# Attention on one Trainium2 core: value products of selected and sliding keys issued in one run, the compressed product last

## The reference

```python
s = jnp.einsum('bqgre,bige->bqgri', qg, kc) * SCALE
p_cmp, _ = _masked_softmax(s, (cmp_last[None, :] <= t[:, None])[:, None, None, :])
o_cmp = jnp.einsum('bqgri,bige->bqgre', p_cmp.astype(vc.dtype), vc)
...
o_slc = jnp.einsum('bqgrk,bqgke->bqgre', p.astype(vs.dtype), vs)
...
o_win = jnp.einsum('bqgrk,bkge->bqgre', p.astype(vw.dtype), vw)
...
o = g[..., 0:1] * o_cmp + g[..., 1:2] * o_slc + g[..., 2:3] * o_win
```

## Time and profile before

| | |
|---|---|
| time, median of 3 runs | 2013.63 us (2011.82 to 2014.28) |
| the profiled execution's own time | 2008.03 us |
| its span, first to last instruction | 2006.2 us |
| mean granted TensorE clock | 0.980 |
| busy share: PE, PEld, DVE, ACT, POOL | 94%, 74%, 52%, 38%, 13% |
| attention, first to last product of TensorE | 451.6 to 1023.5 us of the span |
| passes 8 to 15 | about 655 to 1023 us, 45.0 us each (pass 12: 839.32 to 884.33) |

### The profile page before, as it was taken

The page is one execution under the profiler, slowest core; times in us unless marked ns, Lnnn a source line. Parts: engine busy times, 40 slices in busy tenths (PEclk is TensorE's granted clock), DMA queues, the critical chain, the costliest instruction groups (busy, mean ns, idle before and its releaser), DMA issues. The chain is left out here.

```text
span 2006.2 us, 30543 instructions
## 1 busy us (share of the span) xinstructions
PE 1879.5 (94%) x11675; PEld 1494.0 (74%) x11675; DVE 1044.3 (52%) x2481; ACT 761.9 (38%) x1583; POOL 263.8 (13%) x344
## 2 busy tenths in 40 slices
PE   5997999979999899899969999999999999999997
PEld 4786777977776666666647787787887887887886
DVE  5866881336666666666644435434434434433434
ACT  4444442116777565655542332212212212212211
POOL 1000000004444344443310000000000000000000
PEclk7998999999999999999989999999999999999999
DMA  5334232415655322233352213113113113114102
GB/s 181 108 110 134 87 113 90 160 34 144 176 169 163 99 91 87 90 90 101 100 182 86 63 42 106 63 42 105 63 43 105 63 42 105 64 42 147 41 3 93
DMA packets 171942, 192.09 MB, mean 96 GB/s; under 512 B 55302, under 2 KB 138502, under 8 KB 169528
## 3 DMA queue, kind: packets, MB, share of 16 engines
q1 hardware_dynamic: 169458, 175.56, 28.1%
q0 software_dynamic: 2352, 14.73, 2.2%
HBM read 168.72 MB, written 59.81 MB: 114 GB/s over the span
## 5 line engine op out<-in xcount | busy, mean ns | idle before, releaser
L1847 DVE CUSTOM_DVE_ANT_0 l_e<-l_s,k_masks 128x1024 f32<-128x1024 f32 (+3 forms) x192 | 138.5, 721 | 102.7 <-PE l_s L1492 101.6
L1792 ACT ACTIVATE l_e<-l_e,l_nmin 128x640 f32<-128x640 f32 (+11 forms) x224 | 169.0, 754 | 32.5 <-DVE l_nmin L1847 30.8
L2267 PE MATMUL o_py<-f_h_hi,m_gu_hi 128*128 128x512 f32 x704 | 179.7, 397 | 0.0
L2267 PE MATMUL o_py<-f_h_lo,m_gu_hi 128*128 128x512 f32 x704 | 178.5, 395 | 0.0
L2267 PE MATMUL o_py<-f_h_hi,m_gu_lo 128*128 128x512 f32 x704 | 178.4, 395 | 0.0
L2267 PEld LDWEIGHTS o_py<-f_h_hi,m_gu_lo 128*128 128x128 f32 x704 | 132.1, 188 | 32.2
L2267 PEld LDWEIGHTS o_py<-f_h_lo,m_gu_hi 128*128 128x128 f32 x704 | 132.0, 188 | 32.2
L2267 PEld LDWEIGHTS o_py<-f_h_hi,m_gu_hi 128*128 128x128 f32 x704 | 129.7, 188 | 29.7
L2525 DVE SCALAR_TENSOR_TENSOR a_kv_nat<-m_ext,m_taps,a_kv_nat 128x512 f32<-128x512 f32 x22 | 16.6, 752 | 249.9 <-ACT m_ext L2416 249.9
L1532 PE MATMUL l_t<-k_ident,l_e 128*128 128x128 f32 x816 | 123.7, 276 | 0.5 <-POOL l_e L1439 0.3
L375 PE MATMUL p_pz<-p_whi,p_xhi 128*128 128x512 f32 (+3 forms) x432 | 104.6, 386 | 19.9 <-DVE p_xlo L407 15.7
(11 more groups left out here) (312 smaller groups left out, 3695.9 us busy)
## 6 DMA issues: line engine op xcount, KB each, us to landing
m_raw_gu<-in_w_gate SPq DMA_DIRECT2D x22, 512.0 KB, 5.2
m_raw_gu<-in_w_up SPq DMA_DIRECT2D x22, 512.0 KB, 7.0
m_raw_d<-in_w_down SPq DMA_DIRECT2D x11, 1024.0 KB, 5.0
k_first<-in_w_in SPq DMA_DIRECT2D x5, 2048.0 KB, 8.1
a_kd_k<-in_state_dil SPq DMA_DIRECT2D x8, 1024.0 KB, 8.2
a_kd_v<-in_state_dil SPq DMA_DIRECT2D x8, 1024.0 KB, 7.7
a_kd_k<-in_cache_slc SPq DMA_DIRECT2D x128, 64.0 KB, 1.8
k_w<-in_w POOLq DMA_DIRECT2D x4, 1024.0 KB, 5.6
```

What stands on the lines that cost most here:

```text
L1792: nc.scalar.activation(e, e, ACT.Exp, bias=nmin[0:r, k:k + 1], scale=-1.0, accum_out=total[0:r, k:k + 1]).then_inc(exped, 1)
L1847: return nc.vector.tensor_tensor_reduce(out=dst, in0=src, in1=m, scale=1.0, scalar=CLAMP, op0=ALU.add, op1=ALU.min, accum_out=low)
L2267: last = nc.tensor.matmul(bank[q % 3][:, 0:w], ws[k][:, m, c, :], hs[:, c, t0:t0 + w], start=(j == 0 and c == 0), stop=(j == 2 and c == KC ...
```

## The change

The products of `l` are no longer made in a place of their own. At the place of `w` (stages 8, 13, 17 and 2 of the next pass) TensorE waits for `o_free`, makes the blocks of `l`, then those of `w`, then the compressed product, which ends the group. The number of products is the same. The probabilities of an `l` pair have to wait for three or more stages longer, so `pT` has three slots: `w` has slot 1 for itself, `l` and `d` alternate between 0 and 2. Parts of `pT` that must be zero are cleared by GpSimd at the start of attention (four instructions instead of two), and the later clearing in pass 8 (L1464, one instruction, behind a wait for the last dilated products) is gone. The transfers and all other work are the same.

```diff
-    job, total = {}, {}
+    job, total, slot = {}, {}, {}
...
+            slot[kind, p, j] = 1 if kind == "w" else len(total) % 2 * 2
...
-        pT = sb("l_pT", [P, 2, TILES, 2 * P])
+        pT = sb("l_pT", [P, 3, TILES, 2 * P])
...
-            for k in range(2):
+            for k in range(3):
                 nc.gpsimd.tensor_scalar(pT[:, k, 0, 0:P], ident[:], 0.0, 0.0, ALU.mult, ALU.mult).then_inc(zeroed, 1)
+            nc.gpsimd.tensor_scalar(pT[:, 1, 5, P:2 * P], ident[:], 0.0, 0.0, ALU.mult, ALU.mult).then_inc(zeroed, 1)
...
-                if s == base(HB) + LAG_V:
-
-                    need(pool, pv_done, JOB["d", HB - 1, 2] + 1)
-                    nc.gpsimd.tensor_scalar(pT[:, 1, 5, P:2 * P], ident[:], 0.0, 0.0, ALU.mult, ALU.mult).then_inc(zeroed, 1)
...
-                    if j % 2:
+                    if j % 2 or kind == "l":
                         return
...
+                    kinds = "lw" if kind == "w" else "d"
+                    g = TOTAL[p, j]
+                    if g:
+                        need(pe, o_free, g)
+                    need(pe, zeroed, 4)
+                    for name in kinds:
+                        m, blocks = load_of(name, p), pair_blocks(name, j)
+                        emptied(pe, *(("tr", UNIT[name, p, x], q) for x in (j + 1, j) for q in range(prompt_chunks(UNIT[name, p, x]))))
+                        if j == 6:
+                            need(pe, v_kept, m + 1)
+                        v = v_held[slot_of(m)]
+                        for x, blk in enumerate(blocks):
+                            half = slice(x % 2 * E, (x % 2 + 1) * E)
+                            last = nc.tensor.matmul(o_ps[half, 0:2 * P], v[:, blk, :], pT[:, SLOT[name, p, j], x, :],
+                                                    start=(name == kinds[0] and x < 2), stop=(name == "d" and x >= len(blocks) - 2))
+                        if name != "w":
+                            last.then_inc(pv_done, 1)
+                    if kind == "w":
                         c = UNIT["c", p, 0]
                         emptied(pe, ("tr", c, 0), ("tr", c, 1))
...
+                        nc.tensor.matmul(o_ps[:, 0:2 * P], vc_split[:, (p - HB) // RA, :], pc[:, j * P:(j + 2) * P],
+                                         start=False, stop=True).then_inc(pv_done, 1)
...
-            return JOB[kind, p, j - j % 2] % 2, x + 4 * n, min(4, z - a - 4 * n), j % 2
+            return SLOT[kind, p, j - j % 2], x + 4 * n, min(4, z - a - 4 * n), j % 2
```

More of the change, by code:

```diff
@@ L1173, in pv_jobs @@
             job[kind, p, j] = len(job)
+            slot[kind, p, j] = 1 if kind == "w" else len(total) % 2 * 2
             if kind in "dw":
                 total[p, j] = len(total)
-    return job, total
+    return job, total, slot
 RING = 4
@@ L1194, in attend @@
     AT = {c: key for key, c in CH.items()}
-    JOB, TOTAL = pv_jobs()
+    JOB, TOTAL, SLOT = pv_jobs()
     with ExitStack() as ctx:
@@ L1581, in pv @@
-                    last.then_inc(pv_done, 1)
+                        nc.tensor.matmul(o_ps[:, 0:2 * P], vc_split[:, (p - HB) // RA, :], pc[:, j * P:(j + 2) * P],
+                                         start=False, stop=True).then_inc(pv_done, 1)
                     return
```

## The result

The changed kernel took 2032.31 us (median of 4 runs, 2027.02 to 2034.56), the kernel before 2012.72 us (4 runs, 2010.18 to 2014.28). The ratio is 1.0095, with a 95% interval of 1.0082 to 1.0107: slower by about 1%. The forecast was 2031.2 us, slower. The profiled execution took 2032.16 us against 2008.03, its span 2030.4 us against 2006.2.

What follows compares the result with a forecast made beforehand. TensorE was taken to set the time only in some stretches, VectorE or GpSimd in others. 2.06 us a pass, 16.5 in eight, plus 0.8 and 0.3, gave 2025.6, or 2031.2 on the median's scale; range 2014 to 2038.

Steps and rivals of the forecast that it cites:

- What bounds the kernel: TensorE sets the time in stages 8 to 10 and 16 to 19; in others VectorE or GpSimd does.
- l2 and w2: Stages 0 and 2: 0.05 of l2's 1.02 us kept, w2's 0.81 hidden in a 0.90 wait; net 0.
- l6 and w6: Stages 5 and 8: only 0.43 of 2.42 us kept, w6 grows by 1.67; net +1.24 us a pass.
- l0 and w0: Stages 11 and 13: l0's 0.58 us becomes more wait for VectorE, w0 grows; +0.64 us a pass.
- l4 and w4: Stage 15 and w4's place: 1.06 of 2.43 us kept, w4 adds 1.24; net +0.18 us a pass.
- The sum: A pass 2.06 us longer, eight passes 16.5; with the ends 17.6 us more, 2031.2 on the median's scale.
- Faster: TensorE's issue sets the whole pass, all freed time kept: 2.09 us less a pass, 1997.2 us; chance 0.13.
- No change: VectorE gets ahead in stages 4 and 5, all of l6's 2.42 us kept: 2015.3 us; chance 0.10.
- Slower by less: The 0.69 wait absorbs part of w6's growth: 1.37 us a pass, 2025.7 us, inside the likeliest case's range (chance 0.72).
- The price for a change of shape: Each costs TensorE 0.10 us; merging saves 64, 6.4 us, which alone would give 2007.2 us.

Runs made afterwards that it cites:

- E3: Changed kernel with only the pair of tiles 4 and 5 merged, the other three as in the kernel before: 2014.05 us, ratio 1.0011.
- E8: Kernel before, nothing merged, products of l4 and w0 made one stage later: 2004.89 us against 2012.43, ratio 0.9960.
- E9: Kernel before, nothing merged, l4 and w0 one stage later and w6 two stages later: 2000.74 us against 2014.01, ratio 0.9929.
- E4: Changed kernel with only the pair of tiles 2 and 3 merged, the other three as in the kernel before: 2010.71 us, ratio 0.9992.
- E7: Kernel before without the 16 products of l6 in stage 5, nothing added elsewhere: 2007.52 us against 2012.43, ratio 0.9978.
- E1: Changed kernel with only the pair of tiles 6 and 7 merged, the other three as in the kernel before: 2018.59 us, ratio 1.0032.
- E2: Changed kernel with only the pair of tiles 0 and 1 merged, the other three as in the kernel before: 2017.49 us, ratio 1.0029.
- E11: The changed kernel run again, unedited: 2029.39 us against 2014.01 for the kernel before, ratio 1.0074.
- E6: Changed kernel, all pairs merged, with the compressed product first in its group instead of last: 2029.51 us against 2012.43, ratio 1.0084.
- E5: Changed kernel with no pair merged, only the three slots and the clearings at the start: 2012.39 us against 2012.43, ratio 0.9996.
- E10: Kernel before with l4, w0 and w6 made later, and l2 made right before w2: 2000.98 us against 2014.01, ratio 0.9939.

## Why the prediction was right

**What bounds the kernel.** Right: it is not TensorE's issue as a whole but alternating stretches. E3 removes the wait for the output bank and gains nothing; E8 and E9 remove it as well, by putting the products elsewhere, and gain 0.4% and 0.7%.

**l2 and w2, net 0.** Right: -0.05 in the ledger, -0.10 in E4. The new wait of 0.89 for `l_nmin` is what l2 left, and the wait at the `c` transposes has shrunk from 0.90 to 0.24, as w2's growth fits into it: 0.66 of it was used, with 0.81 forecast.

**l6 and w6, +1.24.** Right in mechanism: 0.43 was to be kept, and the milestones give 0.46, E7 0.39. The growth of w6 was 1.67 by the rows; from the transposes of `sc` to the scores of w0 it is 4.12 us after (868.55 to 872.67), 2.35 before, so 1.77. The compressed product behind a group takes 0.22 us to its successor (872.45 to 872.67), between the 0.13 taken and the bound of 0.28. The prediction read the wrong one of two rows: the first full-shape product behind a half-shape group is the one at 855.62, which takes 0.22, and not the next, which takes 0.13. In the sum this cost nothing, because the score product behind, which paid that price before, is shorter now (0.06 after, 872.67 to 872.73; 0.16 before, 859.99 to 860.15): in the ledger the growth is 1.66, from -0.46 to +1.20. Alone, this pair cost 1.15 (E1). The wait also stands in two places, not in the one that was named: 0.71 at L1530 comes ahead of the 0.89 at L1541.

**l0 and w0, +0.64.** Right: 0.72 in the ledger, 0.73 in E2. None of l0's 0.58 was kept; the wait of 0.69 became 1.17. From the compressed product to `sl` there are 0.31 (882.85 to 883.16) with 0.28 taken, and entering the half shape took 0.17 (from the transposes at 881.31 to the group 0.53, before 0.36) with 0.10 taken.

**l4 and w4, +0.18.** Right: 1.01 kept (1.92 less 0.91) with 1.06 forecast, then 1.09 added with 1.24 forecast; alone +0.18 (E3). The term of w4 was too high: entering the half shape, charged with 0.10, cost nothing here (0.69 us from the transposes of `sl` to the group, before and after), and the first score product behind the group is 0.10 shorter (0.18 instead of 0.28), against which the compressed product took 0.09 more than its 0.13. The new wait is at L1550, 0.74 us, with 0.43 ahead of it at L1530, the transposes of w4.

**The sum.** Pass 12 is 2.00 us longer with 2.06 forecast. The four pairs alone come to 1.15 + 0.73 + 0.18 - 0.10 = 1.96 a pass, so they add up with no interplay. By the times, 0.32 + 0.29 + 0.11 - 0.08 = 0.64%, each known to about 0.12; the change measures 0.74 to 0.95%. From the first scores of `c` in pass 8 to those of pass 15 there are 318.8 us before and 335.8 after: 17.0 more, of which some 3.2 are two of the stretches of a lower clock, so 13.8 or 1.97 for each of seven passes. The clock is the one term that the prediction didn't have. The profiled executions lie further apart (24.1 us) than the medians (19.6): 3.1 us of that had gone by before attention began, and some 4.8 are the lower clock. That the median comes within 1.1 us of the 2031.2 forecast is in part luck: the same kernel took 2029.39 us in E11, 15.4 over the kernel before, so the difference of the medians is known to some 4 us only, and the lower clock is in it without having been in the sum. What bears the prediction out is the ledger.

**The rivals.** *Faster*, all freed time kept, would have needed a pass of 43 us; it took 47. *No change*, all of l6's 2.42 kept, fell with E7 (0.39). *Slower by less* wanted the wait of 0.69 to take up part of w6's growth; it grew to 1.17 instead. The price for a change of shape, which spoke for merging, is real in the rows, but merging saves fewer of them than the 64 that were counted: by the shapes on the timeline five a pass, 40 in all, since l6 follows transposes that have the half shape already (852.14 in the earlier trace rows) and w0 gets two more in front of `sl`. The kernel with 40 fewer is the slower one. No run tests the price by itself: a pass of E6 has as many changes of shape as one of the changed kernel.

## What to carry to other kernels

When engines take turns at being late, the price of an instruction is set by its place: find for each stretch which engine waits for which, and move work into a wait. Moving it behind the instruction that others wait for was tried here only together with such moves, so what that alone is worth isn't shown. Grouping like work saves little if it empties a stretch that waits on something else and fills one that others wait on. A long wait in the list is no promise either: removing it pays only if what comes next on that engine isn't late by the same time.

## What the runs showed of the hardware that was not expected

In passes 11, 13 and 15 of the changed kernel TensorE's granted clock falls from 1.00 to 0.50 (from 2.4 to 1.2 GHz) right behind the longest of the waits that are new in every pass, the 1.17 us (1.47 in pass 15) in front of the scores of w4. The table of stretches has pass 12 first, then the same work in pass 13 (us, busy us and instructions of PE, PEld, DVE, ACT and POOL, PEclk, DMA share, GB/s):

```profile
880.00:883.00 3.00, 3.00 (x23) 2.21 (x23) 1.92 (x6) 2.19 (x5) 1.76 (x2) 1.00 0.00 0
927.00:930.00 3.00, 3.00 (x14) 2.60 (x12) 1.33 (x4) 1.69 (x4) 1.55 (x2) 0.50 0.01 3
```

The timeline of pass 13 has the two ends of that stretch:

```profile
926.67 0.56 PE L1489 MATMUL l_s<-l_late,l_qT 128*128 128x512 f32 x1 [1.17 <-DVE l_nmin L1846]
...
931.53 0.64 PE L1512 MATMUL l_s<-a_kd_T,a_bd_nsa 128*64 128x512 f32 x1
```

From the scores of w4 to those of `sl` there are 4.86 us, where pass 12 takes 3.27 (879.89 to 883.16): 1.6 us each, 4.8 for the three. Pass 13 takes 48.60 us for it. E11 repeats it in the same three passes. The Trainium skill, "TensorE: Matmul & The Clock Gate", section "HAM oscillation", puts falls of the clock in a matrix kernel down to waits for data between its stretches of products. The trace agrees only in so far as the fall follows a wait. The wait alone doesn't decide it: passes 12 and 14 have it as well and keep the full clock, and so do all of E6's passes, with the same 1.17 and a mean granted clock of 1.00 over passes 8 to 15, and all of E2's, with 1.17 to 1.18 (1.46 in pass 15).

Nor do such falls belong to the change. The kernel before has one at 643 to 646 us, just ahead of pass 8 (granted clock 0.57 there), behind a wait of 1.95 us. In passes 8 to 15 E5, which merges nothing, has two, E3 two, and E1, E4, E7 and E9 one each; pass 13 of E1 to E10, from which their passes are read, has none. In E9, the fastest here with E10, the products of l6 in pass 10 take 3.49 us instead of 1.95:

```profile
760.24 3.49 PE L1580 MATMUL l_o<-l_pT,l_v 128*64 128x256 f32 x16
```

The waits ahead of it are 0.92 and 0.58 us, and pass 10 of the kernel before has waits of 0.91 and 0.58 at the same places and keeps its clock. What is particular to the changed kernel is that its three falls come back in the same passes. What else than a wait is needed stays open; no run tried to tell it apart.
